# Two blocks of a sequence model on one core: forget-attention scores of two heads in one group with the recurrence's levels prepared a step earlier, and the first convolution slab multiplied one token tile at a time

## The reference, cut to what matters

```python
# forget-attention ("fox"), 8 heads of 64; F is the running sum of log f
s = einsum('bhqd,bhkd->bhqk', qi, k) * scale + Fi[..., None] - F[:, :, None, :]
p = softmax(where(mask, s, -inf)); out = einsum('bhqk,bhkd->bhqd', p, v)
# recurrence ("hgrn2"), 4 heads of 128: S_t = diag(f_t) S_{t-1} + k_t i_t^T; o_t = S_t^T silu(q_t)
# second block's feed-forward
h2 = rms_norm(x, norm_ffn_pre)
up = causal_depthwise_conv(h2 @ w_up, conv_w, conv_b)      # w_up: 1024 x 5632
g, v = split(up); x = x + rms_norm((gelu(g) * v) @ w_down, norm_ffn_post)
```

## Time and profile before

| What | us |
|---|---|
| median of 3 runs | 897.05 |
| the profiled execution, its own time | 897.39 |
| its span from the first to the last instruction | 895.6 |
| PE busy in it | 887.8 (99%) |
| DVE busy | 606.1 (68%) |
| ACT busy | 490.3 (55%) |
| POOL busy | 113.7 (13%) |

### The profile page before, as it was taken

The page is one execution under the profiler, slowest core; times in us unless marked ns, Lnnn a source line. Parts: engine busy times, 40 slices in busy tenths (PEclk is TensorE's granted clock), DMA queues, the critical chain, the costliest instruction groups (busy, mean ns, idle before and its releaser), DMA issues.

```text
span 895.6 us, 15804 instructions
## 1 busy us (share of the span) xinstructions
PE 887.8 (99%) x6287; PEld 819.0 (91%) x6287; DVE 606.1 (68%) x811; ACT 490.3 (55%) x726; POOL 113.7 (13%) x136
## 2 busy tenths in 40 slices
PE   9999999999999999999999999999999999999997
PEld 9998988988989999888899989999999899999886
DVE  5887866866547666644466538898686788888643
ACT  7786554645646555433373347665644666666432
POOL 5551222200001000000034070001000100000000
PEclk9999999999999999999999999999999999999999
DMA  9969522343634766655547554444556386776541
GB/s 297 323 223 317 193 94 96 106 165 105 236 95 129 233 195 203 203 188 188 188 141 247 188 188 142 141 142 162 180 167 198 95 235 188 192 198 203 203 141 47
DMA packets 135764, 160.66 MB, mean 179 GB/s; under 512 B 4064, under 2 KB 113760, under 8 KB 135456
## 3 DMA queue, kind: packets, MB, share of 16 engines
q1 hardware_dynamic: 133648, 152.83, 53.2%
q0 software_dynamic: 1344, 6.03, 1.9%
q10 hardware_dynamic: 720, 1.06, 0.3%
HBM read 158.86 MB, written 1.05 MB: 179 GB/s over the span
## 4 chain that ended last, share of the span: by engine, by line
PE 96%; ACT 1%; issue 1%; DVE 1%; POOL 0%; DVEq 0%; POOLq 0%; ACTq 0%
PE tb L693 17%; PE tb L695 17%; PE tb L694 17%; PE acc L693 12%; PE acc L695 12%; PE acc L694 12%; PE acc L980 1%; PE tb L937 1%; ACT whi L1318 0%; PE tb L1171 0%; PE acc L1219 0%; PE acc L1201 0%; PE tb L1074 0%; PE tb L1056 0%; PE acc L1074 0%
## 5 line engine op out<-in xcount | busy, mean ns | idle before, releaser
L1860 DVE TENSOR_TENSOR wlo<-raw,whi 128x2048 fp32r<-128x2048 f32 x138 | 318.5, 2312 | 174.9 <-ACT whi L1318 174.5
L1318 ACT ACTIVATE whi<-raw 128x2048 fp32r<-128x2048 f32 x138 | 264.1, 1916 | 177.4 <-PE acc L695 118.3
L693 PE MATMUL tb<-xhi,whi 128*128 128x256 f32 x1192 | 331.9, 278 | 0.2
L695 PE MATMUL tb<-xhi,wlo 128*128 128x256 f32 x1192 | 329.6, 276 | 0.0
L694 PE MATMUL tb<-xlo,whi 128*128 128x256 f32 x1192 | 329.5, 276 | 0.0
L693 PEld LDWEIGHTS tb<-xhi,whi 128*128 128x128 f32 x1192 | 224.1, 188 | 1.3 <-issue 1.1
L694 PEld LDWEIGHTS tb<-xlo,whi 128*128 128x128 f32 x1192 | 224.2, 188 | 0.1
L695 PEld LDWEIGHTS tb<-xhi,wlo 128*128 128x128 f32 x1192 | 224.1, 188 | 0.0
L693 PE MATMUL acc<-whi,hid_hi 128*128 128x512 f32 x128 | 50.0, 390 | 0.0
L695 PE MATMUL acc<-whi,hid_lo 128*128 128x512 f32 x128 | 49.8, 389 | 0.0
L694 PE MATMUL acc<-wlo,hid_hi 128*128 128x512 f32 x128 | 49.8, 389 | 0.0
(11 more groups left out here) (394 smaller groups left out, 1525.2 us busy)
## 6 DMA issues: line engine op xcount, KB each, us to landing
raw<-in_w_in SPq DMA_DIRECT2D x37, 1024.0 KB, 5.2
raw<-in_w SPq DMA_DIRECT2D x32, 1024.0 KB, 5.2
raw<-in_w_up SPq DMA_DIRECT2D x44, 512.0 KB, 4.9
raw<-in_w_down SPq DMA_DIRECT2D x22, 512.0 KB, 4.1
raw<-in_w_xkv SPq DMA_DIRECT2D x8, 1024.0 KB, 5.6
raw<-in_w_out SPq DMA_DIRECT2D x8, 1024.0 KB, 5.0
raw<-in_w_mem_kv SPq DMA_DIRECT2D x4, 1024.0 KB, 5.0
raw<-in_w_xq SPq DMA_DIRECT2D x4, 1024.0 KB, 5.0
```

The costliest lines, as they stand in the source:

```text
L693: pe.matmul(o, a_hi, b_hi, start=start, stop=False)
L695: return pe.matmul(o, a_lo, b_hi, start=False, stop=stop)
L1318: act.activation(whi[:, n % RING, :m], raw[:, n % RING, :m], ACT.Copy).then_inc(hi_ready, 1)
L1860: dve.tensor_tensor(low(n), raw[:, n % RING, :m], whi[:, n % RING, :m].bitcast(F32), ALU.subtract).then_inc(lo_ready, 1)
```

## The change

In the stage of forget-attention and recurrence, PE makes the scores of heads i and i+1 together at even i, in the order: F of both, queries by keys of both, first for 128 keys and then for 256. Each head of a pair has a bank of its own (`fox_bank`). Odd steps have no scores. DVE masks odd heads at the top of their step. `hg_diff` and `hg_exp` of level i+2, not i+1, are done in step i; those of level 2 are in step 0, where `hg_diff(2)` stands between `fox_norm(0)` and `hg_merge(0)`. At the start of the convolution stage the second tile's turn no longer precedes the first slab: PE turns tile 0, does 14 transposes instead of 24, multiplies the first column group by the first four k-tiles of tile 0, turns tile 1, and then does the rest of the slab by tile. The slab has 96 passes of 128 columns in place of 48 passes of 256.

```diff
+        def fox_bank(i):
+            return tb[:, 2, :] if i % 2 == 0 else acc[:, 0, 0, :] if i < 4 else tb[:, 1, :]
...
         def h4_part(t, g):
             if t == 0:
-                bank, s = tb[:, g // 2, :], (g % 2) * T
+                bank, s = tb[:, 2 + g // 2, :], (g % 2) * T
             else:
-                bank, s = acc[:, g // 2, 0, :] if g % 2 else tb[:, 2 + g // 2, :], 0
+                bank, s = acc[:, g, 0, :] if g < 2 else tb[:, g - 1, :], 0
...
             def fox_scores(i):
                 if i == 0:
                     emptied(first["fk"] + 1)
+                    emptied(first["gg"] + 1)
...
-                pe.wait_ge(fox["read"], i) if i else None
-                p0, c = (i % 2) * 64, i // 2
-                for o, s, t in ((tb[:, 2, 0:P], P, 0), (tb[:, 2, P:384], T, 1)):
-                    pe.matmul(o, pick[p0:p0 + 64, i:i + 1].broadcast_to([64, P]), negF[p0:p0 + 64, 0:s], start=True, stop=False)
-                    last = pe.matmul(o, fqT[p0:p0 + 64, c, t * P:t * P + P], fkT[p0:p0 + 64, c, 0:s], start=False, stop=True)
-                last.then_inc(fox["scores"], 1)
+                else:
+                    pe.wait_ge(fox["read"], i)
+                if i == 4:
+                    emptied(first["xk"] + 3)
+                for cut, s, t in ((slice(0, P), P, 0), (slice(P, 384), T, 1)):
+                    for j in (i, i + 1):
+                        p = slice((j % 2) * 64, (j % 2) * 64 + 64)
+                        pe.matmul(fox_bank(j)[:, cut], pick[p, j:j + 1].broadcast_to([64, P]), negF[p, 0:s], start=True, stop=False)
+                    for j in (i, i + 1):
+                        p = slice((j % 2) * 64, (j % 2) * 64 + 64)
+                        last = pe.matmul(fox_bank(j)[:, cut], fqT[p, j // 2, t * P:t * P + P], fkT[p, j // 2, 0:s],
+                                         start=False, stop=True)
+                        if t:
+                            last.then_inc(fox["scores"], 1)
...
+                if i == 8:
+                    pe.wait_ge(fox["read"], 8)
...
-                        emptied(first["gg"] + 1)
+                        pe.wait_ge(fox["read"], 4)
...
-                    fox_scores(i)
+                    if i % 2 == 0:
+                        fox_scores(i)
...
-            for t in range(TT):
-                if t:
-                    keep_clock(24, acc[:, 0, 0, 0:P])
+            def h4_turn(t):
                 pe.wait_ge(nrm["dg"], DG["h4"] + t + 1)
...
-            t_loop("cv", 7, "h4")
-            n = first["cv"] + 21
-            pe.wait_ge(dve_emptied, dve_evacs[n - RING])
-            t_slab(n, XHI["h4"], XLO["h4"], 0)
+            n0 = first["cv"]
+            def first_conv(c, t, pairs):
+                a_hi, a_lo, cut = slab(whi, n0, KT), low_slab(n0, KT), slice(t * P, t * P + P)
+                o, m = tb[:, 0, c * T + t * P:c * T + t * P + P], slice(c * P, c * P + P)
+                for g in pairs:
+                    pe.wait_ge(fil["lo"], FILL["h4"][0] + 4 * t + g + 1)
+                    for k in (2 * g, 2 * g + 1):
+                        last = mm3(o, a_hi[:, k, m], a_lo[:, k, m], XHI["h4"][:, k, cut], XLO["h4"][:, k, cut], k == 0, k == 7)
+                return last
+            h4_turn(0)
+            keep_clock(14, acc[:, 0, 0, 0:P])
+            split_ready(n0)
+            first_conv(0, 0, (0, 1))
+            h4_turn(1)
+            first_conv(0, 0, (2, 3))
+            first_conv(1, 0, range(4))
+            first_conv(0, 1, range(4))
+            first_conv(1, 1, range(4)).then_inc(slab_done, 1)
+            n0 += 1
+            with pe.Fori(0, 7) as i:
+                for u in range(RING):
+                    pe.wait_ge(dve_emptied, i * RING + (dve_evacs[n0 + u] - RING))
+                    t_slab(n0 + u, XHI["h4"], XLO["h4"], (u + 1) % RING, i * RING + (n0 + u + 1))
...
# ACT, in step 7 and in each step i < 7
-                    hg_exp(8)
...
-                    if 2 <= i + 1 < 8:
-                        hg_exp(i + 1)
+                    hg_exp(i + 2)
...
# DVE, fox_mask and the steps
-                dve.tensor_tensor(s, tb[:, 2, 0:384], causal[:, :], ALU.add).then_inc(fox["read"], 1)
+                dve.tensor_tensor(s, fox_bank(i)[:, 0:384], causal[:, :], ALU.add).then_inc(fox["read"], 1)
...
+                if i < 8 and i % 2:
+                    fox_mask(i)
...
-                    fox_mask(i)
+                    if i % 2 == 0:
+                        fox_mask(i)
                     if i == 7:
                         laid(turned_mem, C["norm_mem_2"], (2, 3), 4)
-                        hg_diff(8)
-                    if 2 <= i + 1 < 8:
-                        hg_diff(i + 1)
+                    if 1 <= i < 7:
+                        hg_diff(i + 2)
                     if i:
                         fox_lo(i - 1)
                     fox_norm(i)
+                    if i == 0:
+                        hg_diff(2)
                     hg_merge(i)
```

More of the change, by code:

```diff
@@ L1115, in _ @@
             last_row_slab("h2", chi, clo)
[L1118 to L1126, removed]
             first_slab("h2", 0)
```

## The result

The changed kernel takes 902.51 us (median of 6 runs, 900.99 to 902.90), the kernel before, on the same chip, 897.16 (6 runs, 896.67 to 897.38). The ratio is 1.0056, with a 95% interval of 1.0046 to 1.0066; the medians lie 5.35 us apart, the changed kernel being slower. The forecast was 899.3, from 896.3 to 901.5: the sign was right, and the time lies outside the range. The profiled execution took 900.99 and is the fastest of the six, so it can hold only a part of what the others lost.

A forecast was written before the change was run, and what follows sets the result against it. PE, busy 887.8 of 895.6 us, was taken as the bound. The steps' -1.7 us and the first convolution slab's +4.0 gave +2.3 on 897.05, so 899.3 us, range 896.3 to 901.5.

The forecast's parts named there:

- step 1: Attention and recurrence stage: PE waits for level 0's merge, delayed by the subtraction; costs 1.18 us instead of saving 1.13.
- step 5, Step 7: Attention and recurrence stage, odd step without scores: ACT copies before the split, so the full 1.13 us is saved.
- The second heads: Even steps: the second head's scores run beside the first's; 0.03 us per pair, 0.1 for four, bounds 0 and 3.2.
- part B: First convolution slab by token tile: late turn plus 84 short passes where 48 stood; +4.0 us, bounds -0.4 and +4.6.
- Step 3: Attention and recurrence stage: scores saved, but head 2's values wait for a copy behind the split; 0.70 us saved.
- matmuls keep their program order: Rival, even steps: each head's second float32 pass holds up the other head; +1.3 us, 900.6; pairs without overlap had 0.09.
- The late turn: Convolution start: six passes after the second `xlo` pair and a float32 switch make tile 1's turn 0.33 us late.
- The rival of passes that stream at their own length: First convolution slab: 84 short passes take 4.8 us, a change of -0.4, total 895.0; chance 0.10.
- the 81 ns: First convolution slab: by the skill's distance per matmul, the 84 passes take 6.8 us and the kernel about 897.0, no change.
- The full saving: Rival: step 1's merge and step 3's copy don't stop PE; steps change by -4.4 us, total 896.7; chance 0.10.
- Slower or not: Whole kernel: chances of 0.67 for slower, 0.25 for within 0.2% and 0.08 for faster by over 0.2%.

The follow-up runs named there:

- e5: The whole changed kernel plus 18 unread identity transposes on PE in its stop of step 1; 899.68 us, ratio 1.0029 to the kernel before.
- e3: e1 plus 18 unread identity transposes on PE in its stop of step 1; 896.13 us, ratio 0.9988 to the kernel before.
- e4: e1 with level 0's merge ahead of level 2's subtraction on DVE, and ACT's copies and split reordered; 895.20 us, ratio 0.9985.
- e12: e9 with level 2's merge ahead of the normalisation, subtractions for levels 4 and 5 last, exponentials of levels 3 to 5 a step later; 892.42 us, ratio 0.9949.
- e2: The kernel before with only the diff's changes to the convolution stage; 901.04 us, ratio 1.0044.
- e1: The kernel before with only the diff's changes to the stage of steps, the convolution stage unchanged; 897.53 us, ratio 1.0007.
- e8: e4 with level 0's merge moved ahead of head 0's normalisation on DVE; 897.60 us, ratio 0.9999.
- e9: e8 with level 3's subtraction after normalisation and merge on DVE in step 1, its exponential in step 2 on ACT; 893.76 us, ratio 0.9964.
- e11: The whole changed kernel with e9's order on DVE and ACT; 897.32 us, ratio 1.0006 to the kernel before.
- e7: e4 plus 8 unread identity transposes on PE ahead of step 1's products; 895.26 us, ratio 0.9980.
- e10: e8 plus 15 unread identity transposes on PE in step 2, ahead of head 1's transposes; 894.08 us, ratio 0.9964.

## Why the prediction missed

The step that failed is the price of PE's stop in step 1: the forecast counted it at its length. The missing term is the lower clock behind it, 2.8 us at the median. With the clock held the sum is right, +2.3 forecast and +2.6 measured in e5, but partly by luck: step 5 saved 0.9 less than forecast, and that was mostly made up for by steps 6 and 7 (0.25 more), the second heads (0.1) and part B (0.3 less in the profile).

- **Step 1, where it failed.** The prediction put the products of level 1 at 104.41 and the next slab at 107.47, and counted the stop at its own length: "Step 1 costs 1.18 instead of saving 1.13." With the clock held it is 1.12 and 1.13 (e5, e3). Without, PE goes on at 1.2 GHz after the stop of 1.9 us: 1.4 more in the profiled execution (0.17 against -1.19 at the stage's end, in the table), 2.8 at the median. No term, no rival and no bound of the range held this. The kernel before had nothing to price it by at this place; but the first microseconds showed a PE that comes from idleness and has everything twice as far apart, and the prediction used those rows for part B only. (The granted clock reads 1.00 there, from 0 to 4 and from 4 to 8 us, so that it is the same thing isn't shown.)
- **Step 3:** 0.70 forecast, 0.68 in the profile (2.48 - 1.80), 0.69 in e3. The 0.5 wait for the copy behind the split is the one forecast.
- **Step 5, the second failure.** "In steps 5 and 7 ACT makes the copy before the split, and both save 1.13." Step 7 does (1.28 by its own slabs; steps 6 and 7 together 1.37 to 1.39). Step 5 saves 0.2: the prediction followed the turned probabilities through ACT's queue and not the bank that the next slab needs, which ACT empties behind the same split. Where a step gets shorter, every release that its end depends on must be looked at, not the one that the change names. e4 moved only the split in that step, behind that copy, and saves 1.27 there; the kernels built on it save the same, but for e12 with 0.8 and a stop of 0.2 for the merge in that step.
- **The second heads:** 0.1 for four, bounds up to 3.2. Measured 0: the odd head's records start at most 0.01 after the even head's, 1.50 from transposes to products as before. By the rule of the Trainium skill ("TensorE: Matmul & The Clock Gate", Part 2) that matmuls keep their program order the prediction had estimated a cost of 1.3; these pairs are no more held up than the earlier trace rows.
- **Part B:** +4.0 forecast; 4.0 at e2's median, 3.75 in the profiled changed kernel and in e5. The late turn is 0.3 (708.22 - 708.12 + 0.2; forecast 0.33), the distance 0.112 (forecast 0.109), which makes 9.41 of 9.24; and the first pass follows the turn 0.40 sooner than before, which the forecast had at nothing and whose cause is open. The rival of passes that stream at their own length falls, and with it the sum by the 81 ns that the Trainium skill ("TensorE: Matmul & The Clock Gate", "Back-to-back issue gap") gives for a load and a 128-column matmul: the trace has 112 ns for these float32r passes, and the trace decides. Splitting by token tile also can't win where it seems to: a short pass put into the hole leaves its other half, which costs nearly what the long pass did, so the 12 passes in the hole ahead of the turn relieved nothing.
- **The full saving** of 4.4 was a rival with 0.10. As the change was written it didn't come; in e12 it did, 4.6. The mechanism (scores for nothing in every second step) was worth what the earlier trace rows say (4 x 1.13 = 4.52), though by the sum and not step by step: e12's table has 1.22 in step 1, 1.16 in step 3, 0.81 in step 5 and 1.38 in steps 6 and 7. The orders on DVE and ACT decided whether PE got it.
- **Slower or not:** 0.67 stood on slower, which it is. The range was too narrow upward, since the prediction knew of no way in which a stop costs more than its length.

Open: what decides whether and for how long the clock falls. Stops of 1.9 (e1, the changed kernel), 1.8 (8 of 12 runs of e8), 0.9 (2 of 5 of e9, 3 of 11 of e11) and 0.7 (the profiled e4, and 2 of 11 runs by their mean clock of 0.994) were followed by it; stops of 1.5 in e7, in 11 runs, and of 1.0 ahead of step 6 were not. So the length of the stop alone doesn't decide. Only the profiled executions show the place; for the others the mean clock of the run and e5, e7 and e10, which filled the stops, speak.

## What to carry to other kernels

A stop of TensorE of 1 to 2 us can cost more than twice its length, because what comes after it may run at half the clock for some microseconds, and busy time doesn't show it: look at the granted clock and at the number of records per stretch, and price a forecast stop at its length and at that plus some 3 us. When levels or loads are prepared further ahead, put the new work behind whatever the bound engine is about to wait for (here merge, normalisation, then subtraction: 4.6 us gained in place of nothing). Where one engine's stop is removed, ask which chain ends next to it; twice here the stop only moved along DVE's queue.

## What the hardware showed that I had not expected

- A useful kernel gets faster by useless work: 18 transposes in the stop of step 1 took 2.8 us off the changed kernel, 15 in step 2 took 3.5 off e8.
- After a stop at full clock, the distance of 256-column passes went from 0.113 to 0.21 and stayed there for 3 us (the changed kernel, about 106 to 109.1) to 7 us (e1, 104.1 to 111.0). The clock of e4 fell after a stop of only 0.74, that of e7 stayed after 1.51.
- Passes of 128 float32r columns start 0.112 apart and passes of 256 columns 0.113 to 0.118, both with loads of 128 weight columns.
- Two 64-row matmuls in different partition halves, with separate banks, start within 0.01 us of each other and cost the time of one.
- DVE and POOL together: DVE's subtraction 1.22 to 2.57, its scaling of 256 columns 0.35 to 1.37 (both in e8), POOL's multiplication 1.3 to 2.5.
